# Hybrid recurrent step on one core: modulation and a first HGRN tile moved ahead of the S5 set-up

## What is computed

```python
cs = jax.nn.silu(c)                               # conditioning vectors, 1 + 8 sequences
mod = cs @ p['w_ada'] + p['b_ada']                # 6*D columns
sh1, sc1, gt1, sh2, sc2, gt2 = jnp.split(mod, 6, axis=-1)
h = rms_norm(x, g_mix) * (1.0 + sc1) + sh1        # "modulated" input
z = h @ p['w_in']                                 # 256 S5 | RWKV | 4*256 HGRN | gates
# S5 branch: constants from parameters alone
dt = exp(log_dt); mag = exp(lr * dt)
ar, ai = mag * cos(li * dt), mag * sin(li * dt)   # "angles"; powers, B and C matrices follow
er = einsum(ug, bbr); ...; scan over time; y = einsum(s, c)
```

## Time and profile before

| | |
|---|---|
| median of 3 runs | 2406.82 us (2404.63 to 2408.13) |
| the profiled execution | 2405.45 us |
| its span, first to last instruction | 2403.7 us |
| PE busy | 2266.7 us (94%) |
| DVE busy | 1047.3 us (44%) |
| ACT busy | 395.7 us (16%) |
| POOL busy | 169.5 us (7%) |
| mean granted TensorE clock | 0.976 |

### The profile page before, as it was taken

The page is one execution under the profiler, slowest core; times in us unless marked ns, Lnnn a source line. Parts: engine busy times, 40 slices in busy tenths (PEclk is TensorE's granted clock), DMA queues, the critical chain, the costliest instruction groups (busy, mean ns, idle before and its releaser), DMA issues.

```text
span 2403.7 us, 41526 instructions
## 1 busy us (share of the span) xinstructions
PE 2266.7 (94%) x18489; PEld 1592.7 (66%) x18489; DVE 1047.3 (44%) x1649; ACT 395.7 (16%) x758; POOL 169.5 (7%) x277
## 2 busy tenths in 40 slices
PE   5998999998999999999999996999999999999898
PEld 4565666666566566566556664888885668888566
DVE  5855334252352253253234336566651015665323
ACT  3124121231132132042110002111110001111001
POOL 2610000001001002002000001000000000000000
PEclk8999999999999999999999998999999999999999
DMA  8200132212022020111144321111121231110301
GB/s 307 77 23 9 54 131 86 71 46 56 20 65 61 20 63 24 57 30 53 67 167 145 114 72 53 36 37 37 37 72 63 81 101 43 37 38 23 116 22 73
DMA packets 117089, 161.51 MB, mean 67 GB/s; under 512 B 15442, under 2 KB 86599, under 8 KB 116896
## 3 DMA queue, kind: packets, MB, share of 16 engines
q1 hardware_dynamic: 101120, 132.68, 16.9%
q10 hardware_dynamic: 10992, 15.21, 1.8%
q0 software_dynamic: 4800, 10.97, 1.4%
HBM read 126.24 MB, written 32.59 MB: 66 GB/s over the span
## 4 chain that ended last, share of the span: by engine, by line
PE 89%; DVE 5%; DMA 3%; ACT 1%; issue 1%; SPq 1%; POOL 0%; DVEq 0%; ACTq 0%
PE ps L699 88%; DMA W<-in_w_in_dram 2%; DVE arena L1892 2%; PE ps L703 1%; DVE hT L1892 1%; ACT Y L1633 1%; DVE Y L1895 1%; SPq L405 1%; DVE s5v L1892 0%; SPq L420 0%; DMA arena<-in_state_s_dram 0%; ACT hT L1578 0%; DMA out_dram<-arena 0%; DVE Y L2466 0%; DVE Y L1892 0%
## 5 line engine op out<-in xcount | busy, mean ns | idle before, releaser
L699 PE MATMUL ps<-hT,W 128*128 128x352 f32 (+1 forms) x3312 | 989.8, 449 | 34.8 <-DVE flag L1986 21.3
L699 PEld LDWEIGHTS ps<-hT,W 128*128 128x128 f32 x3312 | 621.2, 193 | 293.6 <-DVE flag L1986 22.5
L699 PE MATMUL ps<-arena,W 128*128 128x352 f32 (+1 forms) x1792 | 515.1, 449 | 15.0 <-DVE arena L1892 11.2
L699 PEld LDWEIGHTS ps<-arena,W 128*128 128x128 f32 x1792 | 343.1, 192 | 183.0 <-DVE arena L1892 12.9
L699 PE MATMUL ps<-arena 64*64 64x64 f32 (+8 forms) x9752 | 407.3, 240 | 36.0 <-issue 19.6
L699 PEld LDWEIGHTS ps<-arena 64*64 64x64 f32 (+4 forms) x9752 | 327.0, 139 | 165.5 <-issue 100.9
L1892 DVE TENSOR_TENSOR arena<-ps,arena 128x512 f32<-128x512 f32 (+4 forms) x124 | 93.2, 751 | 263.2 <-PE ps L699 206.7
L1892 DVE TENSOR_TENSOR arena<-arena 128x1056 f32<-128x1056 f32 (+6 forms) x180 | 165.6, 920 | 62.5 <-PE ps L699 47.6
L1895 DVE SCALAR_TENSOR_TENSOR arena<-ps,MOD,arena 128x352 f32<-128x352 f32 (+1 forms) x72 | 41.3, 573 | 326.8 <-PE ps L699 322.1
L1892 DVE TENSOR_TENSOR Y<-Y,ps 128x528 f32<-128x528 f32 x110 | 77.5, 705 | 216.8 <-PE ps L699 216.8
L1523 ACT ACTIVATE arena<-ps 128x512 f32<-128x512 f32 (+6 forms) x143 | 86.5, 616 | 452.3 <-PE ps L699 254.2
(11 more groups left out here) (282 smaller groups left out, 1269.7 us busy)
## 6 DMA issues: line engine op xcount, KB each, us to landing
W<-in_w_ada_dram SPq DMA_DIRECT2D x12, 2048.0 KB, 9.3
W<-in_w_up_dram SPq DMA_DIRECT2D x22, 1024.0 KB, 6.8
W<-in_w_in_dram SPq DMA_DIRECT2D x13, 1024.0 KB, 6.2
gates<-arena ACTq DMA_DIRECT2D x72, 176.0 KB, 1.8
arena<-gates SPq DMA_DIRECT2D x24, 528.0 KB, 3.6
arena<-xres SPq DMA_DIRECT2D x24, 528.0 KB, 5.2
xres<-arena POOLq DMA_DIRECT2D x16, 528.0 KB, 3.0
W<-in_w_in_dram SPq DMA_DIRECT2D x13, 512.0 KB, 7.4
```

The lines of the kernel that those rows point to most:

```text
L699: return nc.tensor.matmul(out, lhsT, rhs, start=start, stop=stop, skip_group_check=True)
```

## The change

Only the order of instructions changes; none is added and none is taken out. On ScalarE the copies of the `w_ada` products 2 and 3 follow those of 0 and 1, and the modulation follows at once; the S5 functions (Exp, copy, Exp, Exp, and with a table load Sin, Sin) come behind. On VectorE `MOD`, `GSC`, the modulation and `h_ready` come ahead of the S5 angles and of `low` (the lower bound of the HGRN gate). On TensorE the first tile of the HGRN chunk goes ahead of the turns of `BB` and `CRI`. SP's and GpSimd's streams stay as they are.

```diff
@@ TensorE
             for t in range(2):
                 gemm(wslot(i, 0, 8, 256), P * t, 8, h, "z_ev")
 
+            def hg_tiles(c, *tiles):
+                i = index[("hg", c)]
+                arrived(i)
+                for q in tiles:
+                    gemm(wslot(i, 0, 8, 512), P * q, 8, h, "z_ev")
+
+            hg_tiles(0, 0)
             pe.wait_ge(sem("s5_set"), 2)
             for q in range(4):
                 b = 6 + q % 2
...
-            hg_tiles(0, 0, 1, 2, 3)
+            hg_tiles(0, 1, 2, 3)
             pe.wait_ge(sem("s5_set"), 3)
@@ ScalarE
             root(xrs, 1)
             ada_copy(0, 6)
             ada_copy(1, 7)
+            ada_copy(2, 6)
+            ada_copy(3, 7)
...
+            act.wait_ge(sem("xn_ready"), KT)
+            act.wait_ge(sem("gsc_ready"), 1)
+            for k in range(HK0):
+                modulate(0, k)
             act.wait_ge(sem("par_ready"), 1)
             V = lambda k: s5v[:, k, :]
             step(nc.scalar.activation(V(0), par("s5_log_dt", 0, NJ), ACT.Exp))
...
             nc.scalar.activation(V(5), V(2), ACT.Exp).then_inc(sem("s5_fn"), 1)
             nc.scalar.activation(V(6), V(3), ACT.Sin).then_inc(sem("s5_fn"), 1)
             nc.scalar.activation(V(7), V(4), ACT.Sin).then_inc(sem("s5_fn"), 1)
-            ada_copy(2, 6)
-            ada_copy(3, 7)
...
-            act.wait_ge(sem("xn_ready"), KT)
-            act.wait_ge(sem("gsc_ready"), 1)
-            for k in range(HK0):
-                modulate(0, k)
@@ VectorE
             for k in range(KT):
                 step(tt(in_two(hT[:, k, 0:TP]), in_two(xT[:, k, 0:TP]), ps[:, 2:4, :], MUL), "xn_ready")
 
...
+            dve.wait_ge(sem("ada_done"), 4)
+            b_ada = par("b_ada", 0, 16).unsqueeze(2).to_broadcast([P, 16, NSEQ])
+            step(tt(MOD[:, 0:16], pb[0][:, 0:16 * NSEQ].rearrange("p (a b) -> p a b", b=NSEQ), b_ada, ADD), "mod_ready")
+
+            scales(0)
+            for k in range(HK0, KT):
+                x = hT[:, k, 0:TP]
+                step(v.tensor_scalar(x, x, GSC[:, 0, k, 0:1], MOD[:, k, 0:1], MUL, ADD))
+            shifted(0)
             V = lambda k: s5v[:, k, :]
             lr, li = par("s5_lambda_re", 0, NJ), par("s5_lambda_im", 0, NJ)
             dve.wait_ge(sem("s5_fn"), 1)
...
             step(v.tensor_scalar(low[:, 3], low[:, 0], -1.0, 1.0, MUL, ADD))
...
-            dve.wait_ge(sem("ada_done"), 4)
...
-            scales(0)
...
-            shifted(0)
             dve.wait_ge(sem("h_ready"), 1)
 
             dve.wait_ge(sem("s5_fn"), 5)
```

More of the change, by code:

```diff
@@ L1563, in _ @@
             ada_copy(1, 7)
[L1564 to L1573, removed]
             ada_copy(2, 6)
@@ L1592, in _ @@
                 modulate(0, k)
+            act.wait_ge(sem("par_ready"), 1)
+            V = lambda k: s5v[:, k, :]
+            step(nc.scalar.activation(V(0), par("s5_log_dt", 0, NJ), ACT.Exp))
+            nc.scalar.copy(V(1), V(0)).then_inc(sem("s5_fn"), 1)
+            act.wait_ge(sem("s5_angles"), 2)
+            nc.scalar.activation(low[:, 1], low[:, 0], ACT.Exp).then_inc(sem("s5_fn"), 1)
+            act.wait_ge(sem("s5_angles"), 1)
+            nc.scalar.activation(V(5), V(2), ACT.Exp).then_inc(sem("s5_fn"), 1)
+            nc.scalar.activation(V(6), V(3), ACT.Sin).then_inc(sem("s5_fn"), 1)
+            nc.scalar.activation(V(7), V(4), ACT.Sin).then_inc(sem("s5_fn"), 1)
             ring = [0]
@@ L1928, in _ @@
                 step(tt(in_two(hT[:, k, 0:TP]), in_two(xT[:, k, 0:TP]), ps[:, 2:4, :], MUL), "xn_ready")
[L1930 to L1949, removed]
             def scales(n):
@@ L1996, in _ @@
             shifted(0)
+            V = lambda k: s5v[:, k, :]
+            lr, li = par("s5_lambda_re", 0, NJ), par("s5_lambda_im", 0, NJ)
+            dve.wait_ge(sem("s5_fn"), 1)
+            step(tt(V(8), li, V(0), MUL))
+            step(v.tensor_scalar(V(9), V(8), math.pi / 2, None, ADD))
+            for src, dst, tmp in ((8, 3, 10), (9, 4, 11)):
+                step(v.tensor_scalar(V(tmp), V(src), 1 / (2 * math.pi), ROUND, MUL, ADD))
+                step(v.tensor_scalar(V(tmp), V(tmp), ROUND, None, SUB))
+                step(stt(V(12), V(tmp), -TWO_PI_HI, V(src), MUL, ADD))
+                step(stt(V(12), V(tmp), -TWO_PI_LO, V(12), MUL, ADD))
+                step(v.tensor_scalar(V(dst), V(12), PI_SAFE, -PI_SAFE, ALU.min, MAX))
+            step(tt(V(2), lr, V(0), MUL), "s5_angles")
+            lb = par("hg_lb", 0, 2)
+            step(tt(low[:, 0], lb, lb, SUB), "s5_angles")
+            dve.wait_ge(sem("s5_fn"), 2)
+            step(v.reciprocal(low[:, 2], low[:, 1]))
+            step(tt(low[:, 2], low[:, 1], low[:, 2], MUL))
+            step(tt(low[:, 0], low[:, 2], low[:, 2], SUB))
+            step(v.tensor_scalar(low[:, 3], low[:, 0], -1.0, 1.0, MUL, ADD))
             dve.wait_ge(sem("h_ready"), 1)
```

## The result

The first measurement gave a median of 2387.26 us (2384.2 to 2394.3, 5 runs) against 2406.82 us (2402.03 to 2415.96, 5 runs), a ratio of 0.9924 with a 95% interval of 0.9905 to 0.9944. The profiled execution is one of the two longer ones of the five: 2394.24 us with a span of 2392.5, so 11.2 us less than the profiled one of before. The other four took 2384.2, 2385.19, 2387.26 and 2394.3.

What follows compares the result with a forecast made beforehand. TensorE bounds the kernel (89% of the chain), so gains come only where it stands still. Modulation 9.0 + turns 1.15 = 10.15 us off the median 2406.82 gives 2396.7 us, range 2393.0 to 2401.0.

Steps and rivals of the forecast that it cites:

- The modulation, 9.0 us: At the start, `MOD` on VectorE begins at 48.85 instead of 57.85 us, and `h_ready` comes 5.44 us later: 9.0 us gained.
- VectorE, not TensorE or ScalarE, sets the start of `MOD` now: TensorE's columns end by about 46.1 us, ahead of 48.85 where VectorE comes free, so `MOD` starts at 48.85.
- the bound of 48.1 for the columns: Latest end in us of TensorE's sixteen columns at the start if all went at the slow pace, ahead of 48.85.
- The angles, `s5_set` 1 and 2 at 74.9 and 90.2: VectorE's S5 angles now follow `h_ready`; the first two preparation flags come 4.0 us earlier, not 9.0.
- The 4.9 us at the turns without the tile: TensorE going to the turns right behind the two S5 tiles, at 85.4 us, would stand 4.9 us for `s5_set` 2.
- The turns, 1.15 us: VectorE, idle by then, copies the first turned `BB` 0.70 us behind TensorE's arrival instead of 1.85: 1.15 us saved.
- The slack: `s5_set` 3 and 4 come 4 us later, TensorE wants them 10.1 us earlier; slack falls to 17.3 and 9.8 us, costing nothing.
- The clock: TensorE's first projection group loses 2.7 us to the lower clock as before; bounds 2.7 us more gained, 2.0 us less.
- The sum and the range: Whole kernel: 9.0 + 1.15 = 10.15 us gained, 2396.7 us against the median, range 2393.0 to 2401.0.
- The part-gain rival: Turns save nothing, first group wholly at the lower clock, loss behind the turns twice: gain 5.4 us, 2401.4; chance 0.12.
- The gain is eaten further on: A wait not hanging on TensorE ends at the same time as before, TensorE stands about 10 us: 2406.8; chance 0.06.
- Slower: VectorE's preparation becomes the bound at E; 24.8 us longer makes the kernel 0.2% slower, 2411.6 us; chance 0.03.

Runs made afterwards that it cites:

- the second measurement: The changed kernel again, no edit, against the kernel before: median 2394.38 us (12 runs), ratio 0.9960 (0.9947 to 0.9973).
- its copy: The kernel before run again, unchanged, as a yardstick for the spread: 2402.55 us (12 runs), ratio 0.9990 (0.9976 to 1.0003).
- The repeats: The changed kernel measured twice more, no edit, against the kernel before: 2394.38 us, ratio 0.9960 (12 runs), and 2391.46 us, 0.9952 (6 runs).
- the version with both fillers: The changed kernel plus unread TensorE products, four at the small inputs and eight behind the last columns: 2391.14 us (6 runs), ratio 0.9942.

## Why the prediction was right or wrong

*The modulation, 9.0 us.* Right in place and nearly in size. `MOD` starts at 49.10, 50.50 and 49.47 in the changed kernel's three profiles (49.5 and 49.2 in those with more preparation), against 57.85 and 57.82: 8.1 us in the mean of the three. All three are later than 49, which the prediction had named as a sign of being wrong. The 5.44 us behind it are 5.44 again (49.10 to 54.54).

*"VectorE, not TensorE or ScalarE, sets the start of `MOD` now."* True in all three profiles of the changed kernel, but VectorE's own time hangs on TensorE one step earlier: its multiplies of `hT` begin when TensorE's products by ones end. In the second measurement these were late:

```profile
35.56 4.34 PE L699 MATMUL ps<-arena,ones 128*128 128x128 f32 x18
```

The kernel before took 3.75 us for them, from 34.50 on. They end at 38.50, 39.90 and 38.87 us in the three profiles of the changed kernel against 38.25 in the prediction's profile, 0.8 us later in the mean, and that is the part of the 9.0 us that is missing. And the bound of 48.1 for the columns was not one. It had slowed only the last columns. When TensorE is at the lower clock during the third and fourth product as well (3.64 us each instead of 1.92), the columns end at 51.7 and `MOD` waits 2.38 us for them, as the profile without the tile move shows. In the kernel before the same slow products cost nothing: its copy had 3.64 us for both, the wait for ScalarE behind them was 5.14 us instead of 10.21, and `MOD` came at 57.82 as ever.

*The angles, `s5_set` 1 and 2 at 74.9 and 90.2.* Right: 75.16 and 90.52. The 4.9 us at the turns without the tile: 5.88 measured.

*The turns, 1.15 us.* Right in place: the pause fell from 1.51 us, or 0.94 in the copy, to 0.42. From the start of the projection to the short kernels the changed kernel took 91.9 us in the mean of three against 93.8 in the mean of two, 1.9 us less. The sum had kept the loss of clock behind the turns; it is gone in the changed kernel, and was 1.2 us in one profile of before and nothing in the other.

*The slack.* The cover held, but its size was wrong: 17 us measured, 9.8 forecast. VectorE's output matrices took 24.0 us (100.77 to 124.74) instead of 30.3, and the sum had moved them as a block. GpSimd's tables end earlier relative to them, and the last four instructions ahead of `s5_set` 3 show what that does. VectorE, in the kernel before and in the changed one:

```profile
117.26 2.29 DVE L1892 TENSOR_TENSOR arena<-arena 64x512 f32<-64x512 f32 x1
119.59 2.28 DVE L1895 SCALAR_TENSOR_TENSOR arena<-arena 64x512 f32<-64x512 f32 x1
121.90 2.26 DVE L2095 COPY arena<-arena 64x128 f32<-64x128 f32 x1
124.20 2.28 DVE L2096 TENSOR_SCALAR arena<-arena 64x128 f32<-64x128 f32 x1
```

```profile
122.00 0.69 DVE L1893 TENSOR_TENSOR arena<-arena 64x512 f32<-64x512 f32 x1
122.72 1.44 DVE L1896 SCALAR_TENSOR_TENSOR arena<-arena 64x512 f32<-64x512 f32 x1
124.20 0.22 DVE L2096 COPY arena<-arena 64x128 f32<-64x128 f32 x1
124.45 0.22 DVE L2097 TENSOR_SCALAR arena<-arena 64x128 f32<-64x128 f32 x1
```

GpSimd's table work (L613 to L618) goes on to 126.39 in the first case and ends at 121.88 in the second. The same four instructions take 9.1 us beside it and 2.6 us behind it, a difference of 6.5 us, as much as the whole by which the output matrices were shorter. No run moved GpSimd's work alone, so the cause rests on these rows.

*The clock.* The same loss was taken for the first group, and its size was misread. The prediction held 7.44 us from the group's start to its emptying against 4.73 between two emptyings, but at 2.4 GHz a first group takes 5.04 from start to emptying (104.11 to 109.15 in the changed kernel). So the kernel before lost 2.4 us in front and 1.2 behind the turns, not 2.7 and 1.55. The changed kernel took 45.57, 45.47 and 44.64 us for nine groups that take 42.87 at the higher clock, so it lost 1.8 to 2.7 us in front and nothing behind the turns.

*The sum and the range.* Up to the short kernels the sum is right, 10.1 us of 10.1, though with some luck: the modulation gave 8.1 us instead of 9.0, and the stretch behind it 1.9 instead of 1.15. The step that failed is the last one of the sum, from one profile to the median. It took the median of three runs as the level of the kernel before, and its allowance of 3.7 us either way had 2.0 us for the clock of one group and 1.7 us, half the spread of these three, for all other chance. In fact single executions of the kernel before lie between 2397.4 and 2416.0 us over 77 runs, 18.6 us apart, those of the changed kernel between 2384.2 and 2401.1 over 23, and a median of five can be off by several us. In the profiles the rest behind the edited stretch varies most (2241.0 to 2246.7 us in the changed kernel, against 146.4 to 148.2 up to the cut). The repeats, at 0.9960 and 0.9952, show that most of what the 19.6 us had beyond the sum did not come back. Of the pooled difference of 12.5 us, give or take 1.9, 10.1 are seen in the profiles, and the other 2.4 are a little more than the uncertainty; by the repeats alone it is 11.4, and 10.1 is within it. Whether a small part is a real gain behind the short kernels stays open; the profiles' rests of 2241 to 2247 us against 2245 to 2246 don't decide it. The pooled ratio of 0.9948 puts the level at 2394 when it is applied to the median of 2406.82, inside the range.

*The rivals.* The part-gain rival rested on the turns saving nothing, and they saved 0.5 to 1.1 us. What was said for it, that every pause of TensorE in the trace is followed by slow matmuls, is not so: behind the 1.54 us ahead of E the granted clock is 1.00 (158 to 172 us). "The gain is eaten further on" did not happen. "Slower" was to cancel the gain at 20 us more of preparation and to cost 0.2% at 24.8; with 28.4 us more (135.8 to 164.22) the kernel came to 1.0013 of before (0.9997 to 1.0030), no difference. The mechanism is the right one, and the gain is used up near 17 + 10 = 27 us, an estimate from the slack and the gain in the profiles.

## What to carry to other kernels

When an engine's program is fixed in order, look for the instruction on which it stands and for what is written behind it; here two copies of 0.53 us behind a 17.7 us wait held up TensorE. Moving them paid fully only when the consumer's order was changed along with it (4 us alone, 10 to 12 with the rest), and when TensorE had other work to do in place of a new wait: the same HGRN tile was worth 1 to 3 us in the profiles alone and about 7 beside the earlier modulation. And before the range for a time is set, take the spread from many executions: three runs that agree within 3.5 us said nothing about the 18.6 us that single executions span. A change of what stands beside an engine can change its own time, too: the preparation on VectorE got shorter by being moved against GpSimd's work.

## What the runs showed of the hardware

Executions of the same program differ by up to 18.6 us of 2405, and the mean granted clock of TensorE goes with it at about 1.8 us per 0.001; but that mean also counts pauses, and the version with both fillers lists 0.981 to 0.983 without being faster for it. The fourth `w_ada` product was 1.92 us in one execution and 3.64 in another, at the same place in the program. With a filler of 5.4 us in a pause of TensorE the next group ran at 2.4 GHz in both profiles that have it; four products in an earlier pause were followed by slow ones all the same. Four VectorE instructions took 9.1 us while GpSimd worked on its tables and 2.6 us when it had ended.
